# Attention 1: one 512-column value product per key block and head, collected into one burst per head pair

## The chip, the cores and the metric

The kernel runs on one core of one Trainium2 chip. The metric is device time in microseconds of one whole execution. Beside it stands one profiled execution, from which all durations below come.

## What is computed

The reference is one step of a two-layer transformer trunk. Layer 0 mixes tokens with multi-head latent attention, layer 1 with grouped-query attention; a mixture of experts follows each. The change touches layer 0's attention alone, cut here to its core:

```
def block_attention(q, k, v, scale):
    ...
    def one_block(qblk):
        s = jnp.einsum('bqhgd,bkhd->bhgqk', qblk, k).astype(jnp.float32) * scale
        p = jax.nn.softmax(s, axis=-1).astype(v.dtype)
        return jnp.einsum('bhgqk,bkhe->bqhge', p, v)
...
def mla_attend(q_nope, q_pe, keys, w_uk, w_uv, w_o):
    """Absorbed MLA: keys (B,Tk,KV_DIM) = [c_kv | k_pe] shared by all heads; values = c_kv."""
    ...
    k = keys[:, :, None, :]
    v = keys[:, :, None, :KV_LORA]
    o = block_attention(q, k, v, MLA_SCALE)[:, :, 0]
    o = jnp.einsum('bthc,chv->bthv', o, w_uv).reshape(B, T, MLA_HEADS * MLA_V)
    return o @ w_o
```

`qblk` holds 128 queries. The kernel first turns the latents into values per head (with `w_uv`), so the value product of a head has 64 numbers per key. There are 16 heads, 128 prompt tokens that see 128 keys, and 512 latent tokens that see 640 keys (five blocks of 128). Everything is float32.

## The kernel before

The queries come in five tiles of 128: tile 0 is the prompt, tiles 1 to 4 are the latents. Attention of layer 0 walks 80 steps. A head pair has ten of them, numbered here 0 to 9: two heads for each of the five tiles, so steps 0 and 1 are the prompt tile, 2 and 3 the first latent tile, and so on. There are eight pairs.

The softmax of a step is spread over three engines and two further steps. PE (TensorE) writes the scores (L1994); DVE takes the maximum (`peak`, L1139); ACT takes the exponential (`exp`, L721); DVE divides by the sum (`normalize`, L1146 and L1148). Two steps later PE transposes the result into one shared PSUM place (L1666), and ACT copies it to SBUF (L733). PE's program order is fixed: at step s it issues the scores of s, the transposes of s-2, a `hook`, and at even s a `pair`. The hook makes the next pair's keys and queries in PSUM bank 7 (`MAKE_AT`: keys, L1950, at steps 0 and 1; queries, L1957, at steps 3, 6, 7 and 8) and, at steps 2 and 9 (`ADA_AT`), one slice of layer 1's modulation (`ada`, L1686). `spare_free` waits until ACT and DVE have emptied bank 7 (ACT's part for keys is `key_out`, L771). ACT's part for a slice is `mod_out`: a copy (L693), then two DMA issues (L697).

`pair` is the value product (L1769). For one query tile and both heads of a pair it multiplies transposed probabilities, 128 columns at a time, by 64 columns of values, for every key block: 10 instructions for a latent tile, 2 for the prompt. The two heads of a pair write the lower and the upper 64 partitions of one PSUM bank, so each instruction uses one half of the array's columns. In the trace each float32 matmul appears as two passes, so 10 instructions are 20 rows. We call the ten instructions of one latent tile a group. Its results come from steps two earlier, so tile 1 is due at step 6, tile 2 at step 8, tile 3 at step 0 of the next pair and tile 4 at step 2 of the next pair. The prompt's two instructions are due at step 4.

After the last group DVE copies the result (`latent_out`, L1128), and PE starts the output projection (`mix`, L1741), which needs the weights `w_wo0` and `w_wo1`. At the same time ACT fetches two gate rows (L715) and layer 1's first modulation sums (`mod_fetch`, L709 and L712); DVE finishes these (L1058 to L1062), and PE transposes them (`turn_mods`) between the projections of tiles 0 and 1.

SP's queue issues weight loads in program order. The slices of layer 1's modulation alternate between two SBUF places, slots 0 and 1. `w_wo0` is loaded before attention, `w_wo1` in the second last pair, the first two experts' weights (L485) after the last slice is made.

Of the kernel before, what the change touches and what calls it, by code (L numbers as in the profile page):

```python
# [96 lines left out]


Q_TURN_AT = (0, NTILE + 1)

NQ, NK = HEADS * HD, KVH * HD
SCALE = (QD ** -0.5, HD ** -0.5)
# [77 lines left out]
def program(nc, ctx, A, O):  # L180
# [98 lines left out]
    xn = [lambda t, o=o: ar(o + (t % 2) * D, D) for o in (21120, 23040)]  # L279
    hT = [lambda t, o=o: ar(o + (2 + t % 2) * D, D) for o in (21120, 23040)]  # L280
    Pb = ar(17280, 2 * LKEYS)
    PT = ar(18560, 4 * LKEYS)

    W_PT = ((ar(18944, NB * QW), ar(18944 + NB * QW, NB * QW)), (ring(12288, NB * QW), ring(12288 + NB * QW, NB * QW)))
    W_PP = ring(12288 + 2 * NB * QW, 2 * P)
# [39 lines left out]
        keys = step(s)[3]  # L325
        return 4 * BANK if s % 2 == 0 else 6 * BANK if keys == P else 6 * BANK - P

    def ptbuf(s, n):
        return PT[:, (s % 4) * LKEYS:(s % 4) * LKEYS + n]

    def pt_out_g(s):

# [4 lines left out]
        return split(W_PT[half][h % 2], NB)[:, :, at * P:(at + 1) * P]  # L337


    PV0 = PAIR * NTILE  # L340
    CTX, HALF = 1, (2, 3)

    def wide_done(m, part):
        return PV0 + 3 * m + part
# [17 lines left out]
    def half_bank(half):  # L362
        return bank(7, QW, half * QW)

    def oT_out(it):

        return bank(7, P) if it == 0 else bank(6, P, (it - 1) * P)

    def oT_block(l, m, it, n=1):
        at = m * TOK + it * P  # L370
        return oT[l][:, at:at + n * P]
# [3 lines left out]
        return bank(6 + j % 2 if j < ADA_0 else 7, ADA_ITEMS[j][2])  # L375

    def ada_slot_of(j):
        return ADA_SLOT[j] if j < ADA_0 else (j - ADA_0) % 2

    def ada_at(j):  # L380

# [86 lines left out]
    def _(sp):  # L468
# [59 lines left out]

        def experts(l):

            load_gu(l, 0)
            if l:
                sp.wait_ge(S("qk_ready"), NTILE + 2)
                rows_e_in(1)
                sp.wait_ge(S("pv_done"), wide_done(PAIR - 1, HALF[1]))
            load_gu(l, 1)
            sp.wait_ge(S("mixed"), NTILE * (l + 1))
            load_dn(l, 0)
            load_gu(l, 2)
            load_dn(l, 1)  # L540
            load_dn(l, 2)
            if l == 0:
                mod_fetch(1, 1)
            sp.wait_ge(S("h_ready"), NTILE * (l + 1))
            for v in range(2):
                sp.dma_start(gate_m[:, v * D:(v + 1) * D], modrow[l][v, 5:6, :].broadcast_to([P, D])).then_inc(S("gates_m"), 16)
            sp.wait_ge(S("routed"), l + 1)
            for e in range(NE - RING_N):
                end = end_of(e)
                sp.wait_ge(S("gu_done", l), end)  # L550
                load_gu(l, e + RING_N)
# [27 lines left out]
            load_ada(j)  # L579
        sp.wait_ge(S("ada_made"), 1 + max(j for j in range(ADA_0) if ada_slot_of(j) in (3, 4)))  # L580
        load(S("uq_landed"), w_uq, A["mla_w_uq"], 3)
        sp.wait_ge(S("ada_made"), ADA_0 - 2)
        load(S("wo_landed", 0), w_wo0, A["mla_w_o"][0], KD)
        for j in range(ADA_0, ADA_ALL):
            load_ada(j)
            if j == ADA_0 + 1:
                mod_fetch(0, 1)
            if j == ADA_0 + 3:
                mod_store(0)
        sp.wait_ge(S("made"), len(MAKES) * PAIR)  # L590
        load(S("wo_landed", 0), w_wo1, A["mla_w_o"][1], KD)
        rows_e_in(0)
# [72 lines left out]
    def _(act):  # L665
# [58 lines left out]
        def heads(hook):  # L724

            for s in range(STEPS + 2):
                if s >= 2:
                    j = s - 2
                    keys = step(j)[3]
                    act.wait_ge(S("p_turned"), j + 1)  # L730
                    if j >= 4:
                        act.wait_ge(S("pv_done"), (j - 4) // 2 + 1)
                    act.activation(ptbuf(j, keys), ps[:, 4 * BANK:4 * BANK + keys], ACT.Copy).then_inc(S("pt_ready"), 1)  # L733
                if s < STEPS:
                    exp(0, s)
                    hook(0, *divmod(s, PER_PAIR))
# [304 lines left out]
    def _(dve):  # L1041
# [77 lines left out]

        def prompt_out(l, m):  # L1120

            dve.wait_ge(S("pv_done"), wide_done(m, CTX) if l else m * NTILE + 1)
            nc.vector.tensor_copy(oT_block(l, m, 0), bank(7, P)).then_inc(S("oT_prompt"), 1)

        def latent_out(m):

            dve.wait_ge(S("pv_done"), m * NTILE + NTILE)
# [534 lines left out]
    def _(pe):  # L1662
# [92 lines left out]

        def heads(score, v_of, hook):

            def pair(p):

                m, it = divmod(p, NTILE)  # L1760
                blocks, first = (1, 5) if it == 0 else (LKEYS // P, 0)
                pe.wait_ge(S("pt_ready"), 2 * p + 2)
                if it == 0:
                    spare_free(m, PROMPT_AT)
                if m and it == 1:
                    pe.wait_ge(S("oT_latent"), m)
                for j in range(blocks):
                    for odd in range(2):
                        last = mm(oT_out(it)[VD * odd:VD * (odd + 1)], v_of(2 * m + odd, first + j),  # L1769
                                  ptbuf(2 * p + odd, blocks * P)[:, j * P:(j + 1) * P], start=j == 0, stop=j == blocks - 1)  # L1770
                last.then_inc(S("pv_done"), 1)

            for s in range(STEPS + 4):
                if s < STEPS:
# [14 lines left out]
                if s >= 4 and s % 2 == 0:  # L1789
                    pair((s - 4) // 2)  # L1790

        def heads_g(score, v_of, last_turns):

# [531 lines left out]
```

## Time and profile before

| | |
|---|---|
| median of three runs | 1293.39 us (1291.4 to 1294.76) |
| profiled execution | 1292.7 us, of which span 1290.9 us |
| PE busy | 1231.8 us, 95% of the span |
| attention of layer 0 | from about 138 to 392 us |
| TensorE clock granted there | 1.00 of full speed |

The span runs from the first to the last instruction of the profiled execution; the execution's own time is 1.8 us more. A row of the timeline merges neighbouring instructions of one line on one engine; its second number is how long they are busy, and the start of the following row says when the engine went on.

### The profile page before, as it was taken

What the parts mean: (1) busy time and instruction counts of PE and PEld (TensorE: products, weight loads), DVE (VectorE), ACT (ScalarE), POOL (GpSimd) and SP (SyncE); (2) the same over time, 40 slices, a digit from 0 to 9 for tenths busy, and PEclk for the clock granted to TensorE, in tenths of its full rate; (3) what the DMA queues carried; (4) which work ended last, traced back from release to release, by engine and by line L of the source; (5) the groups of instructions that cost most, each with busy time, mean ns of one, the idle gap of its engine ahead of it and who ended that gap; (6) DMA issues with size and microseconds to landing.
All of it is one profiled execution on the core that took longest, in us unless ns stands there. A gap on an engine that the chain in (4) does not pass through costs nothing.

```text
span 1290.9 us, 17251 instructions
## 1 busy us (share of the span) xinstructions
PE 1231.8 (95%) x5561; PEld 681.9 (53%) x5562; DVE 589.3 (46%) x1338; ACT 409.8 (32%) x855; POOL 58.2 (5%) x63
## 2 busy tenths in 40 slices
PE   7999999999999999998978999799999999999997
PEld 4554566666664475443434444466654574444443
DVE  1322455555552574322228544888735663322216
ACT  2332344444451121111022325677732111111122
POOL 0103000000000020000002000000000110000002
PEclk9999999999999999999998999899999999999999
DMA  9979999622244057999987000600020279999947
GB/s 373 414 312 407 414 413 410 259 100 100 100 186 165 33 202 244 355 355 356 364 313 267 9 1 9 256 1 1 2 99 0 102 274 317 355 293 334 352 183 265
DMA packets 88357, 290.18 MB, mean 225 GB/s; under 512 B 9209, under 2 KB 27580, under 8 KB 86876
## 3 DMA queue, kind: packets, MB, share of 16 engines
q1 hardware_dynamic: 46032, 185.68, 39.4%
q0 software_dynamic: 16640, 64.59, 12.7%
q10 hardware_dynamic: 25612, 38.96, 8.9%
q8 instruction: 42, 0.69, 0.2%
q14 instruction: 31, 0.25, 0.1%
HBM read 214.48 MB, written 74.73 MB: 224 GB/s over the span
## 4 chain that ended last, share of the span: by engine, by line
PE 80%; DMA 6%; DVE 5%; ACT 3%; SPq 3%; issue 2%; ACTq 1%; DVEq 1%; POOL 0%; POOLq 0%
PE ps L2114 16%; PE ps L1724 11%; PE ps L1741 10%; PE ps L2143 7%; PE ps L1666 7%; PE ps L1994 6%; PE ps L1957 4%; PE ps L1769 3%; PE ps L2193 3%; PE ps L1818 3%; PE ps L1686 2%; DMA arena<-in_moe_gu 2%; PE ps L2056 2%; PE ps L1950 2%; PE ps L1967 2%
## 5 line engine op out<-in xcount | busy, mean ns | idle before, releaser
L2114 PE MATMUL ps<-arena 128*128 (+1 forms) x560 | 247.7, 595 | 0.0
L2114 PEld LDWEIGHTS ps<-arena 128*128 128x128 f32 x560 | 104.5, 191 | 118.1 <-issue 118.0
L1666 PE MATMUL ps<-const,arena 128*128 128x128 f32 (+2 forms) x1000 | 145.4, 279 | 18.0 <-DMA const<-in_const 8.2
L1724 PE MATMUL ps<-arena 128*128 128x512 f32 (+2 forms) x400 | 152.1, 535 | 4.6 <-DVE arena L1246 1.2
L1666 PEld LDWEIGHTS ps<-const,arena 128*128 128x128 f32 (+2 forms) x1000 | 115.8, 142 | 76.6 <-issue 39.8
L1139 DVE TENSOR_REDUCE hst<-ps 128x1 f32<-128x640 f32 (+1 forms) x160 | 110.9, 714 | 94.0 <-PE ps L1994 80.1
L1741 PE MATMUL ps<-arena 128*128 128x512 f32 x320 | 142.0, 597 | 1.4 <-issue 1.4
L2143 PE MATMUL ps<-arena 128*128 (+1 forms) x280 | 126.1, 593 | 2.2 <-ACT arena L844 2.2
L721 ACT ACTIVATE arena<-ps,hst 128x640 f32<-128x640 f32 (+1 forms) x160 | 112.4, 706 | 42.0 <-DVE hst L1139 42.0
L1724 PEld LDWEIGHTS ps<-arena 128*128 128x128 f32 x400 | 74.4, 190 | 74.1 <-issue 58.1
L1741 PEld LDWEIGHTS ps<-arena 128*128 128x128 f32 x320 | 59.1, 190 | 69.8 <-issue 69.7
L1994 PE MATMUL ps<-arena 128*128 128x320 f32 (+1 forms) x288 | 90.3, 432 | 1.4 <-issue 1.4
L2143 PEld LDWEIGHTS ps<-arena 128*128 128x128 f32 x280 | 53.0, 190 | 68.7 <-issue 68.7
L733 ACT ACTIVATE arena<-ps 128x640 f32<-128x640 f32 (+1 forms) x80 | 49.4, 618 | 120.6 <-PE ps L1666 112.8
L1148 DVE TENSOR_SCALAR arena<-arena,hinv 128x640 f32<-128x640 f32 (+1 forms) x160 | 80.0, 500 | 13.1 <-issue 0.9
L831 ACT ACTIVATE arena<-ps 128x256 f32<-128x256 f32 x35 | 13.4, 383 | 226.5 <-PE ps L2114 207.3
L1549 DVE STREAM_TRANSPOSE arena<-arena 128x1024 f32<-128x1024 f32 x31 | 62.9, 2028 | 35.9 <-DMA arena<-slot_rows 35.9
L1555 DVE TENSOR_TENSOR arena<-ps,arena 128x256 f32<-128x256 f32 x35 | 14.8, 422 | 132.9 <-ACT arena L831 132.9
L1994 PEld LDWEIGHTS ps<-arena 128*128 128x128 f32 x288 | 50.0, 189 | 28.5 <-issue 13.7
L844 ACT ACTIVATE arena<-ps 128x1024 f32<-128x1024 f32 x33 | 33.8, 1023 | 96.1 <-PE ps L2143 96.1
L2193 PE MATMUL ps<-arena 64*128 64x320 f32 (+1 forms) x288 | 54.2, 458 | 6.1 <-ACT arena L721 5.5
L1957 PE MATMUL ps<-arena 128*128 128x320 f32 x192 | 57.0, 433 | 0.0
(218 smaller groups left out, 1173.9 us busy)
## 6 DMA issues: line engine op xcount, KB each, us to landing
arena<-in_moe_gu SPq DMA_DIRECT2D x128, 512.0 KB, 13.1
arena<-in_ada_w SPq DMA_DIRECT2D x62, 768.0 KB, 11.9
slot_rows<-arena POOLq DMA_DIRECT2D x10, 4096.0 KB, 67.7
arena<-in_moe_w_down SPq DMA_DIRECT2D x64, 512.0 KB, 16.1
slot_rows<-arena ACTq DMA_DIRECT2D x33, 512.0 KB, 8.5
arena<-slot_rows ACTq DMA_DIRECT2D x124, 128.0 KB, 13.4
arena<-mod_rows SPq DMA_DIRECT2D x12, 512.0 KB, 12.3
arena<-in_gqa_w_qkv SPq DMA_DIRECT2D x12, 512.0 KB, 13.7
```

The costliest lines, as they stand in the source:

```text
L721: act.activation(split(pbuf(l, s, keys), 2 if keys > P else 1), scores(s, keys), ACT.Exp, bias=hst[:, b:b + 1], accum_out=hsum[:, b:b + 1] ...
L1139: nc.vector.tensor_reduce(hst[:, b:b + 1], scores(s, step(s)[3]), AX.XY, ALU.max, negate=True)\
L1148: nc.vector.tensor_scalar(pbuf(l, j, keys), pbuf(l, j, keys), hinv[:, b:b + 1], None, ALU.mult)\
L1549: nc.vector.transpose(e_xsT[:, c].rearrange("p (k r b) -> p k r b", k=KD, b=XB), e_xs[:, c].rearrange("p (r a k) -> p k r a", k=KD, a=XB)) ...
L1666: return nc.tensor.transpose(out, in_, ident[0:rows, 0:rows])
L1724: last = mm(bank(2 + b, cols), hT[l](t)[:, k * P:(k + 1) * P], w[:, k], start=k == 0, stop=k == KD - 1)
L1741: last = mm(bank(mix_bank(it) + half), oT_block(l, k, it), w[:, k], start=k == 0, stop=k == KD - 1)
L1957: last = mm(bank(7, QCH), w[:, k, h * P:(h + 1) * P], m_qlT[:, at:at + QCH], start=k == 0, stop=k == 2)
L1994: last = mm(scores(s, keys)[:, c], m_qT[:, at:at + P], m_kT[:, k:k + w], start=True, stop=True)
L2114: last = mm(bank(gu_bank(u)), e_xsT[:, nth(u, D)][:, k * P:(k + 1) * P], w(k * BANK, BANK), start=k == 0, stop=k == KD - 1)
L2143: last = mm(bank(6 + n), e_hidT[:, nth(u, FF)][:, k * P:(k + 1) * P], w(k * D + n * BANK, BANK), start=k == 0, stop=k == 1)
L2193: last = mm(scores(s, keys)[:, c], g_qT[half, q:q + P], g_kT[half, at:at + w], start=True, stop=True)
```

## The change

The four latent tiles of a pair share one product. ACT writes the transposed probabilities of the four tiles beside each other, so that a key block of one head is 512 columns (`pt_out_m`, buffers `M_PT` and `M_PP`). PE then issues ten instructions of 512 columns for the pair, all at step 2 of the next pair, in place of four groups of ten with 128 columns at steps 6, 8, 0 and 2. The prompt's two instructions stay at step 4. ACT's copies wait for the previous pair's product.

The second buffer takes SBUF that was slot 0. So the slices use slots 2 and 1, `w_wo0`, which lies on slot 2, is loaded after the last slice there, and the first experts' weights wait for the last value product.

```diff
+LATENTS_AT = ((2, 0, NB),)
...
-    PT = ar(18560, 4 * LKEYS)
+    M_PT, M_PP = (ar(18560, NB * BANK), ring(10240, NB * BANK)), ring(12800, 2 * P)
...
+    def pt_out_m(s):
+
+        m, it, h, keys = step(s)
+        if it == 0:
+            return M_PP[:, (h % 2) * P:(h % 2 + 1) * P]
+        return split(M_PT[h % 2], NB)[:, :, (it - 1) * P:it * P]
...
-        return ADA_SLOT[j] if j < ADA_0 else (j - ADA_0) % 2
+        return ADA_SLOT[j] if j < ADA_0 else 2 - (j - ADA_0) % 2
...
+            if l == 0:
+                sp.wait_ge(S("pv_done"), PV0)
             load_gu(l, 0)
...
-        sp.wait_ge(S("ada_made"), ADA_0 - 2)
-        load(S("wo_landed", 0), w_wo0, A["mla_w_o"][0], KD)
...
+        sp.wait_ge(S("ada_made"), 1 + max(j for j in range(ADA_ALL) if ada_slot_of(j) == 2))
+        load(S("wo_landed", 0), w_wo0, A["mla_w_o"][0], KD)
...
-                    if j >= 4:
-                        act.wait_ge(S("pv_done"), (j - 4) // 2 + 1)
-                    act.activation(ptbuf(j, keys), ps[:, 4 * BANK:4 * BANK + keys], ACT.Copy).then_inc(S("pt_ready"), 1)
+                    if m:
+                        act.wait_ge(S("pv_done"), latent_done(m - 1) if it else prompt_done(m - 1))
+                    turned = ps[:, 4 * BANK:4 * BANK + keys]
+                    act.activation(pt_out_m(j), split(turned, NB) if it else turned, ACT.Copy).then_inc(S("pt_ready"), 1)
...
-            def pair(p):
...
+            def latents(m, first, end):
+
+                if first == 0:
+                    pe.wait_ge(S("pt_ready"), (m + 1) * PER_PAIR)
+                    if m:
+                        pe.wait_ge(S("oT_latent"), m)
+                for j in range(first, end):
                     for odd in range(2):
-                        last = mm(oT_out(it)[VD * odd:VD * (odd + 1)], v_of(2 * m + odd, first + j),
-                                  ptbuf(2 * p + odd, blocks * P)[:, j * P:(j + 1) * P], start=j == 0, stop=j == blocks - 1)
-                last.then_inc(S("pv_done"), 1)
+                        last = mm(bank(6)[VD * odd:VD * (odd + 1)], v_of(2 * m + odd, j), M_PT[odd][:, j * BANK:(j + 1) * BANK],
+                                  start=j == 0, stop=j == NB - 1)
+                if end == NB:
+                    last.then_inc(S("pv_done"), 1)
```

PE's order changes at steps 6, 8, 0 and 2. Here are its instructions from the scores of step 8 to the group at step 0 of the next pair, before (64x128 is a group):

```order
L1994 MATMUL ps<-arena 128x320 x2
L1666 MATMUL ps<-const,arena 128x128 x5
L1957 MATMUL ps<-arena 128x320 x3
L1769 MATMUL ps<-arena 64x128 x10
L1994 MATMUL ps<-arena 128x320 x2
L1666 MATMUL ps<-const,arena 128x128 x5
L1686 MATMUL ps<-arena,cond 2x384 x8
L1994 MATMUL ps<-arena 128x128
L1666 MATMUL ps<-const,arena 128x128 x5
L1950 MATMUL ps<-arena 128x384 x2
L1769 MATMUL ps<-arena 64x128 x10
```

The same stretch in the changed kernel, with its own line numbers:

```order
L2015 MATMUL ps<-arena 128x320 x2
L1676 MATMUL ps<-const,arena 128x128 x5
L1978 MATMUL ps<-arena 128x320 x3
L2015 MATMUL ps<-arena 128x320 x2
L1676 MATMUL ps<-const,arena 128x128 x5
L1696 MATMUL ps<-arena,cond 2x384 x8
L2015 MATMUL ps<-arena 128x128
L1676 MATMUL ps<-const,arena 128x128 x5
L1971 MATMUL ps<-arena 128x384 x2
```

The groups behind the queries of step 8 and behind the keys of step 0 are gone, so the next scores follow the makes directly. At PE's step 2 the row of the last group was this, between the slice and the scores of step 3:

```order
L1994 MATMUL ps<-arena 128x320 x2
L1666 MATMUL ps<-const,arena 128x128
L1686 MATMUL ps<-arena,cond 2x384 x8
L1769 MATMUL ps<-arena 64x128 x10
L1994 MATMUL ps<-arena 128x320 x2
```

And in the changed kernel:

```order
L2015 MATMUL ps<-arena 128x320 x2
L1676 MATMUL ps<-const,arena 128x128
L1696 MATMUL ps<-arena,cond 2x384 x8
L1785 MATMUL ps<-arena 64x512 x10
L2015 MATMUL ps<-arena 128x320 x2
```

The ten instructions stay where they were and become four times as wide; they now hold all four latent tiles of the previous pair.

On SP's queue, the end of the attention part before is this (the last slice, the second half of the output weights, modulation rows, the router, the experts' weights):

```order
L473 DMA arena<-in_ada_w 128x1536
L474 DMA arena<-in_ada_w 128x1536
L473 DMA arena<-in_mla_w_o 128x2048
L474 DMA arena<-in_mla_w_o 128x2048
L526 DMA arena<-mod_rows 128x1024 x4
L527 DMA rw<-in_moe_router 128x256
L485 DMA arena<-in_moe_gu 128x1024 x8
```

And in the changed kernel:

```order
L480 DMA arena<-in_ada_w 128x1536
L481 DMA arena<-in_ada_w 128x1536
L480 DMA arena<-in_mla_w_o 128x2048
L481 DMA arena<-in_mla_w_o 128x2048
L480 DMA arena<-in_mla_w_o 128x2048
L481 DMA arena<-in_mla_w_o 128x2048
L533 DMA arena<-mod_rows 128x1024 x4
L534 DMA rw<-in_moe_router 128x256
L492 DMA arena<-in_moe_gu 128x1024 x8
```

Both halves of the output weights now stand behind the last slice, and the wait for the last value product stands ahead of the experts' weights.

## Rows read from the trace of the kernel before

**Rows 1.** The page: busy time, share of the span and instructions of PE.

```profile
PE 1231.8 (95%) x5561; PEld 681.9 (53%) x5562; DVE 589.3 (46%) x1338; ACT 409.8 (32%) x855; POOL 58.2 (5%) x63
```

**Rows 2.** Windows, middle and last pair; columns: length, PE, PEld, DVE, ACT, POOL, clock, DMA.

```profile
264.44:296.76 32.32, 32.32 (x230) 21.68 (x227) 16.68 (x38) 14.97 (x36) 0.00 (x0) 1.00 0.28 100
361.44:391.93 30.49, 27.82 (x249) 19.02 (x245) 14.90 (x35) 16.17 (x37) 0.00 (x0) 1.00 0.65 237
```

**Rows 3.** Waits in that middle pair: total us, times, longest.

```profile
ACT arena L733 <- PE ps L1666: 16.2, 10, 3.2
```

**Rows 4.** Timeline of PE, steps 7 and 8 of a pair.

```profile
255.02 1.78 PE L1957 MATMUL ps<-arena 128*128 128x320 f32 x6
256.64 1.24 PE L1994 MATMUL ps<-arena 128*128 128x320 f32 x4
...
258.26 1.78 PE L1957 MATMUL ps<-arena 128*128 128x320 f32 x6
259.97 1.31 PE L1769 MATMUL ps<-arena 128*64 128x128 f32 x20
261.21 1.34 PE L1994 MATMUL ps<-arena 128*128 128x320 f32 x4
```

**Rows 5.** Timeline of PE: 64-row products of 128 and 256 columns, full ones of 512.

```profile
246.40 0.44 PE L1769 MATMUL ps<-arena 128*64 128x128 f32 x4
...
406.52 14.00 PE L1741 MATMUL ps<-arena 128*128 128x512 f32 x32
...
421.23 3.60 PE L1741 MATMUL ps<-arena 128*128 128x512 f32 x8
...
826.08 1.52 PE L1818 MATMUL ps<-arena 128*64 128x256 f32 x12
...
830.05 1.08 PE L1818 MATMUL ps<-arena 128*64 128x256 f32 x8
```

**Rows 6.** Timeline of PE and ACT, steps 9, 0 and 1.

```profile
265.09 1.00 ACTq L697 DMA_DIRECT2D mod_raw<-arena  x2
266.20 0.70 ACT L733 ACTIVATE arena<-ps 128x640 f32<-128x640 f32 x1 [1.14 <-PE ps L1666]
266.78 1.31 PE L1769 MATMUL ps<-arena 128*64 128x128 f32 x20
267.14 0.47 ACT L771 ACTIVATE arena<-ps 64x384 f32<-64x384 f32 x1
268.89 1.46 PE L1950 MATMUL ps<-arena 128*128 128x384 f32 x4
```

**Rows 7.** Timeline of PE, last pair: slice of step 2, scores of steps 5 to 7.

```profile
365.93 1.47 PE L1686 MATMUL ps<-arena,cond 128*2 128x384 f32 x16
...
372.61 1.34 PE L1994 MATMUL ps<-arena 128*128 128x320 f32 x4
...
374.33 1.24 PE L1994 MATMUL ps<-arena 128*128 128x320 f32 x4
...
377.51 1.34 PE L1994 MATMUL ps<-arena 128*128 128x320 f32 x4
```

**Rows 8.** The chain that ended last, from 384 to 410 us: start, us, what.

```profile
387.39 0.71 ACT arena L733
...
388.24 0.76 PE ps L1666 x5
...
389.77 1.34 PE ps L1769 x20
...
394.05 10.23 DMA mod_vec<-in_vec_m
...
406.35 0.24 PE ps L1666
```

**Rows 9.** SP's timeline, and DMA issues from 361 to 405 us with landing times.

```profile
385.76 5.99 SPq L485 DMA_DIRECT2D arena<-in_moe_gu  x8
...
arena<-in_mla_w_o SPq DMA_DIRECT2D x2, 1024.0 KB, 9.3
```

More of the change, by code:

```diff
@@ L326, in turned_at @@
         return 4 * BANK if s % 2 == 0 else 6 * BANK if keys == P else 6 * BANK - P
-    def ptbuf(s, n):
-        return PT[:, (s % 4) * LKEYS:(s % 4) * LKEYS + n]
+    def pt_out_m(s):
[3 more added lines that the diff above has]
+        return split(M_PT[h % 2], NB)[:, :, (it - 1) * P:it * P]
     def pt_out_g(s):
@@ L337, in pt_out_g, with prompt_done, latent_done @@
         return split(W_PT[half][h % 2], NB)[:, :, at * P:(at + 1) * P]
-    PV0 = PAIR * NTILE
+    PV0 = 2 * PAIR
     CTX, HALF = 1, (2, 3)
+    def prompt_done(m):
+        return 2 * m + 1
+    def latent_done(m):
+        return 2 * m + 2
     def wide_done(m, part):
@@ L363, in half_bank @@
         return bank(7, QW, half * QW)
-    def oT_out(it):
-        return bank(7, P) if it == 0 else bank(6, P, (it - 1) * P)
     def oT_block(l, m, it, n=1):
@@ L728, in heads @@
                     j = s - 2
-                    keys = step(j)[3]
+                    m, it, _, keys = step(j)
                     act.wait_ge(S("p_turned"), j + 1)
-                    if j >= 4:
-                        act.wait_ge(S("pv_done"), (j - 4) // 2 + 1)
-                    act.activation(ptbuf(j, keys), ps[:, 4 * BANK:4 * BANK + keys], ACT.Copy).then_inc(S("pt_ready"), 1)
+                    if m:
+                        act.wait_ge(S("pv_done"), latent_done(m - 1) if it else prompt_done(m - 1))
+                    turned = ps[:, 4 * BANK:4 * BANK + keys]
+                    act.activation(pt_out_m(j), split(turned, NB) if it else turned, ACT.Copy).then_inc(S("pt_ready"), 1)
                 if s < STEPS:
@@ L1120, in prompt_out @@
         def prompt_out(l, m):
-            dve.wait_ge(S("pv_done"), wide_done(m, CTX) if l else m * NTILE + 1)
+            dve.wait_ge(S("pv_done"), wide_done(m, CTX) if l else prompt_done(m))
             nc.vector.tensor_copy(oT_block(l, m, 0), bank(7, P)).then_inc(S("oT_prompt"), 1)
         def latent_out(m):
-            dve.wait_ge(S("pv_done"), m * NTILE + NTILE)
+            dve.wait_ge(S("pv_done"), latent_done(m))
             nc.vector.tensor_copy(oT_block(0, m, 1, LAT), bank(6)).then_inc(S("oT_latent"), 1)
@@ L1756, in heads, with prompt @@
         def heads(score, v_of, hook):
-            def pair(p):
[L1760 to L1767, printed above, removed]
+            def prompt(m):
+                pe.wait_ge(S("pt_ready"), m * PER_PAIR + 2)
+                spare_free(m, PROMPT_AT)
+                for odd in range(2):
+                    last = mm(bank(7, P)[VD * odd:VD * (odd + 1)], v_of(2 * m + odd, NKEYT - 1), M_PP[:, odd * P:(odd + 1) * P],
+                              start=True, stop=True)
+                last.then_inc(S("pv_done"), 1)
[5 more added lines that the diff above has]
+                for j in range(first, end):
                     for odd in range(2):
-                        last = mm(oT_out(it)[VD * odd:VD * (odd + 1)], v_of(2 * m + odd, first + j),
-                                  ptbuf(2 * p + odd, blocks * P)[:, j * P:(j + 1) * P], start=j == 0, stop=j == blocks - 1)
-                last.then_inc(S("pv_done"), 1)
+                        last = mm(bank(6)[VD * odd:VD * (odd + 1)], v_of(2 * m + odd, j), M_PT[odd][:, j * BANK:(j + 1) * BANK],
+                                  start=j == 0, stop=j == NB - 1)
+                if end == NB:
+                    last.then_inc(S("pv_done"), 1)
             for s in range(STEPS + 4):
@@ L1788, in heads @@
                     hook(*divmod(s, PER_PAIR))
-                if s >= 4 and s % 2 == 0:
-                    pair((s - 4) // 2)
+                m, r = divmod(s, PER_PAIR)
+                if m < PAIR and r == PROMPT_AT:
+                    prompt(m)
+                for at, first, end in LATENTS_AT:
+                    if m and r == at:
+                        latents(m - 1, first, end)
         def heads_g(score, v_of, last_turns):
```

## The prediction

> **What bounds the kernel now.** I read the page first: PE is busy for 95% of the span [rows 1], so the question for attention 1 is whether PE's time there is work or waiting. The windows answer it. In a middle pair PE is busy for all of 32.32 us while DVE has 16.68 and ACT 14.97 [rows 2]. Pairs 1 to 6 read alike in the timeline, step by step. The waits say the same from the other side: in that pair ACT's copies alone waited 16.2 us for PE's transposes [rows 3]. So in pairs 0 to 6 a microsecond less of PE is a microsecond less of time, until one of the softmax steps behind it becomes late. The last pair is another matter: it makes no keys or queries for a successor, and PE is busy for 27.82 of the 30.49 us up to the projection [rows 2]. Its end is a chain of single steps, read below from the chain of waits.
>
> **What a group costs.** A group of 20 passes begins at 259.97, and the scores behind it begin at 261.21: 1.24 us. That is not all. The same six passes of a query make take 1.62 us until the next instruction starts when scores follow (255.02 to 256.64), and 1.71 us when a group follows (258.26 to 259.97). The scores take 1.34 us behind a group and 1.24 us behind a make [rows 4]. So 0.09 us ahead and 0.10 us behind also belong to the group; I take 1.43 us as what disappears with it.
>
> **What the burst costs.** The trace has no 64-row product of 512 columns, so I bound it from three widths. At 128 columns 20 passes are busy 1.31 us [rows 4] and 4 passes 0.44 us [rows 5]: 0.87 us for 16 more, or 0.109 us for two passes (one of each head, side by side in the two halves of the array). At 256 columns 12 passes take 1.52 and 8 take 1.08: 0.22 us for two. A full-width pass of 512 columns takes (14.00 - 3.60) / 24 = 0.433 us [rows 5]. The cost is proportional to columns, and two half-width passes cost one full one. So ten steps of two passes grow by 10 x (0.43 - 0.109) = 3.21 us, and the burst takes 1.24 + 3.21 = 4.45 us. From below, four times 0.109 would give 4.50; a price of 0.22 doubled gives 4.55, an excess of 3.31. I keep 3.21. The slice is ahead of it and the scores are behind it as before, so no edge is added.
>
> The columns therefore cost the same: four groups stream as much as one burst. What is gained is three sets of edges. Each group spends 1.24 - 10 x 0.109 = 0.15 us of its own on starting and ending, plus 0.19 on its neighbours, 0.34 together. The Trainium skill (TensorEngine Tiling, Tiling Modes, Key Properties) says that changing the tiling mode drains the engine; TensorE: Matmul & The Clock Gate (Part 2, step by step) puts a drain at some 128 cycles, as an estimate 0.05 us at 2.4 GHz, which for a change on either side would be 0.11 us a group in place of 0.34. The rows decide here.
>
> **Where the removed groups stood.**
> - Steps 6 and 8 of pairs 0 to 6: 14 groups, each behind a query make, with the next step's make behind them. That make needs bank 7 emptied by DVE, and the next scores (1.24) and transposes cover that copy (a like one of ACT takes 0.47 [rows 6]). 14 x 1.43 = 20.0 us.
> - Step 0 of pairs 1 to 6: 6 groups, behind the first key make. Here something waits. ACT issues two stores of the slice of step 9 until 266.09, so its copy of step 8 starts only at 266.20, and its `key_out` ends at 267.61. PE's second key make needs that, and starts at 268.89 now [rows 6]. Without the group it would be ready at 268.89 - 1.43 = 267.46; ACT and a hand-over of under 0.1 us allow it at about 267.7. So 1.2 us comes back, 0.2 turns into a wait: 6 x 1.2 = 7.2 us. Bounds: 1.43 each if ACT catches up, 0.9 if the transposes ahead wait as well.
> - Step 0 of pair 7: no keys are made, and the transposes of step 9 wait for the same late copy. Nothing.
> - Steps 6 and 8 of pair 7: step 5, without a group, takes 372.61 to 374.33 = 1.72 us, and step 6 with one 374.33 to 377.51 = 3.18 [rows 7]. If steps 6 to 9 run at 1.7 to 1.75, the two groups give 2.8 us; DVE with 14.90 us and ACT with 16.17 in this window of ten steps [rows 2] need 1.5 and 1.6 us a step, so they just keep up.
> - The groups at steps 0 and 2 behind the last pair. ACT's copy of step 78 starts at 387.39, held up by the stores of the last slice; the transposes of step 79 start at 388.24, and the last product at 389.77 [rows 8]. Tile 3's group lay inside that wait: removing it gives nothing. The last product becomes the burst.
>
> **The sum.** Gains: 20.0 + 7.2 + 2.8 = 30.0 us. Bursts: seven at step 2 of pairs 1 to 7 and one at the end, 8 x 3.21 = 25.7 us. Net -4.3 us.
>
> **What moves and costs nothing.** The burst holds PE for 4.45 us; behind it wait only scores of step 3 and transposes whose inputs are long ready, and DVE's `latent_out` stands at step 4. ACT's new wait (for the previous burst) is on copies of step 2, whose transposes PE issues at step 4, behind the burst. The wider stride of ACT's copy has its like in layer 1: same 128x640 elements there, no dearer. Both halves of the output weights now leave SP after the slice at step 2 of the last pair. That slice begins at 365.93 and takes 1.5 us [rows 7], the projection begins at 391.93 [rows 2]; with the burst in between and the last pair's gain off, some 25 us are left. One half took 9.3 us to land [rows 9]; two behind each other, under 20. The experts' weights (385.76 now) start 5.4 us later against the last product's end (389.77 + 1.34 [rows 8]); they are first multiplied behind all five projection tiles of 14.00 us [rows 5].
>
> What has least room is the fetch behind the last product: its last piece is issued at 394.05 and takes 10.23 us; the small transposes at 406.35 come behind it, 0.45 us after PE ran dry [rows 8]. In the changed kernel the eight loads of experts' weights, 5.99 us of issuing [rows 9], start together with it and no longer ahead of it. Either can win: from -0.45 (fetch sooner, no wait) to +5.4 us (fetch behind all of them). I take no change, since both queues share the engines now too.
>
> The profiled execution took 1292.7, so -4.3 gives 1288.4; the median of the runs shown is 0.7 above it, so **1289.1 us**.
>
> **Rivals.**
> - *The edges aren't saved.* If the 0.34 us belongs to the neighbours' own rhythm, a removed group gives 1.09: 14 x 1.09 + 6 x 0.9 + 2 x 1.05 = 22.8 against 25.7, time about 1296.3. Against: scores and makes without a group show no such edge [rows 4]. That is within 0.3% of before. Chance 0.12. With the Trainium skill's drains (the estimate above, 0.11 us for each of the 22) it would be about 1294.
> - *The fetch falls behind the experts' weights.* 5.4 us later than now would make it 1294.5; half of that 1291.8. Within 0.3%. Chance 0.10.
> - *Slower: the groups were cover for the softmax.* Removing them shortens steps 7, 9 and 1 against the chain maximum, exponential, scaling, transposes, copy. If that chain is late by w in each of the 22 places that count, the sum is -4.3 + 22 w; it is nil at w = 0.20 and slower by over 0.3% from w = 0.37, for instance w = 0.5 gives 1300. For: step 1 shows such a lateness. Against: at steps 7 and 9 a make or a slice of 1.4 to 1.6 us remains, and DVE and ACT are idle half the pair [rows 2]. Chance 0.04.
> - *Slower: the output weights land late*, which takes under 170 GB/s for 4.2 MB in 25 us; one half alone needed 9.3 us in company [rows 9]. At 120 GB/s PE waits 10 us: 1299. Chance 0.02.
>
> **How the numbers follow.** The forecast's mechanism has the remaining 0.72. Within it the bounds are: 1.43 at step 0 (-1.4) and no fetch wait (-0.45) below, 1285 to 1287; the dearer burst (+0.8) and 0.9 at step 0 (+1.8) above, 1291.7. The range, with the runs' own spread of some 1.5 us, is 1285.5 to 1292.5; it leaves out the first rival's upper part and the slower ones. 0.3% of 1293.4, about what a measurement of this kernel can tell from no change, is 3.9 us, so the line stands at 1289.5 and the forecast lies just past it. Of the 0.72 I give 0.56 to faster and 0.16 to the same; with the rivals: faster 0.56, same 0.39, slower 0.05.
>
> **What would show it.** Right: pair length 32.3 falls to about 31.5; the 20 passes of 512 columns take 4.4 to 4.5 us; scores of steps 7 and 9 take 1.24 us; a wait of 0.1 to 0.3 us for ACT ahead of the second key make; PE idle for most of the 1.3 us that tile 3's last group filled. Wrong: new waits at steps 7 to 9, a pass pair far from 0.43, or a wait over 1 us at the small transposes between the first two projection tiles.

## The result, and the profile after

The changed kernel is slightly slower. Its median is 1295.2 us (1293.5 to 1298.1, 8 runs) beside 1292.1 us for the kernel before (8 runs): ratio 1.0026, 95% interval 1.0016 to 1.0036. Run again later it gave 1296.1 against 1291.8: 1.0031 (1.0022 to 1.0040). The forecast was 1289.1, its range 1285.5 to 1292.5: wrong. The profiled execution took 1293.8 us, span 1292.0.

PE's line of the page beside [rows 1]: 480 matmuls and 480 weight loads less, 6.0 us less busy, and a span 1.1 us longer.

```profile
PE 1225.8 (95%) x5081; PEld 660.6 (51%) x5082; DVE 589.7 (46%) x1338; ACT 410.3 (32%) x855; POOL 58.3 (5%) x63
```

The windows answer to [rows 2]: from step 2 to step 2 of the next pair, first an early pair, then the one that now holds [rows 2]'s stretch, then the last pair up to the projection (length, PE, PEld, DVE, ACT, POOL, clock, DMA share, GB/s):

```profile
167.96:200.28 32.32, 31.57 (x167) 19.06 (x166) 16.76 (x38) 14.99 (x34) 0.00 (x0) 1.00 1.02 413
264.17:295.72 31.55, 31.55 (x168) 19.06 (x167) 16.67 (x38) 14.99 (x34) 0.00 (x0) 1.00 0.29 100
...
359.55:390.06 30.51, 26.60 (x137) 12.73 (x130) 12.46 (x27) 13.12 (x27) 0.00 (x0) 0.94 0.56 216
```

The later pair fell from 32.32 to 31.55 us, as forecast. The early one did not fall at all: PE is busy for 31.57 us and waits for 0.75. And the last one ran at a mean granted clock of 0.94.

PE's timeline in the later pair shows the burst, and at its end two query makes with scores directly behind them:

```profile
265.45 1.48 PE L1696 MATMUL ps<-arena,cond 128*2 128x384 f32 x16
266.85 4.51 PE L1785 MATMUL ps<-arena 128*64 128x512 f32 x20
271.30 1.34 PE L2015 MATMUL ps<-arena 128*128 128x320 f32 x4
...
284.71 1.24 PE L2015 MATMUL ps<-arena 128*128 128x320 f32 x4
...
286.33 1.78 PE L1978 MATMUL ps<-arena 128*128 128x320 f32 x6
287.95 1.24 PE L2015 MATMUL ps<-arena 128*128 128x320 f32 x4
```

The burst holds PE for 271.30 - 266.85 = 4.45 us, the forecast's number. A make takes 287.95 - 286.33 = 1.62 us and the scores 1.24, without the 0.09 and 0.10 that a group cost its neighbours [rows 4].

The early pair, ACT and PE from step 9 to step 1 (compare [rows 6]):

```profile
163.22 1.81 ACTq L706 DMA_DIRECT2D mod_raw<-arena  x2
...
165.08 0.70 ACT L743 ACTIVATE arena<-ps 128x640 f32<-128x640 f32 x1 [1.89 <-issue]
...
165.93 0.74 PE L1676 MATMUL ps<-const,arena 128*128 128x128 f32 x5 [0.71 <-ACT arena L743]
...
166.03 0.47 ACT L781 ACTIVATE arena<-ps 64x384 f32<-64x384 f32 x1
...
166.60 1.53 PE L1971 MATMUL ps<-arena 128*128 128x384 f32 x4
```

ACT spends 1.81 us on issuing the slice's two stores, so its copy starts late and PE's transposes wait 0.71 us. The kernel before has this row too, in the early pair that [rows 6] does not show:

```profile
168.11 1.84 ACTq L697 DMA_DIRECT2D mod_raw<-arena  x2
```

In the later pair of the changed kernel the same two stores take 1.03 us:

```profile
260.16 1.03 ACTq L706 DMA_DIRECT2D mod_raw<-arena  x2
261.29 0.70 ACT L743 ACTIVATE arena<-ps 128x640 f32<-128x640 f32 x1 [1.16 <-PE ps L1676]
```

The windows suggest what differs: the DMA engines are full in the early pair (share 1.02, 413 GB/s) and at 0.29 in the later one. Around the stores themselves (160 to 166 and 258 to 264 us) the share is 1.03 and 0.57. Pairs 1 to 3 are all like the early one and pairs 4 to 6 all like the later one, in both kernels; no run changed the DMA load alone, so that it is the cause is not shown.

The end of attention, in the chain that ended last (start, us, what), answers to [rows 8]; behind it PE's timeline with its two waits, and the clock of the last burst's stretch (columns as in the windows above):

```profile
380.65 0.71 ACT arena L743
...
381.50 0.75 PE ps L1676 x5
...
382.27 0.71 ACT arena L743
...
383.03 6.19 PE ps L1785 x20
389.22 0.84 issue
390.06 13.97 PE ps L1751 x32
404.03 0.17 PE ps L1676
```

```profile
381.50 0.74 PE L1676 MATMUL ps<-const,arena 128*128 128x128 f32 x5 [1.84 <-ACT arena L743]
383.03 1.98 PE L1785 MATMUL ps<-arena 128*64 128x512 f32 x4 [0.79 <-ACT arena L743]
```

```profile
383.03:389.31 6.28, 6.19 (x20) 1.71 (x20) 0.04 (x1) 0.00 (x0) 0.00 (x0) 0.73 0.00 0
```

The last burst took 6.19 us where its like takes 4.51. The granted clock fell to the lower of its two levels (1.2 GHz) at 383.03, for part of the burst (0.73 over the stretch). What went ahead of it on PE is a wait of 1.84 us, 0.74 us of transposes and a wait of 0.79 us. The small transposes at 404.03 follow the projection at once: the fetch that was to have least room was in time.

From the first score to the projection, attention took 253.75 us, against 253.61 before. So the result is not made in attention alone: three microseconds stand at the end of the program. There POOL gathers the experts' rows while the last are still being stored, DVE scales what was gathered by its weight, and PE sums it. From PE's first sum to its last this took 31.75 us, where it had been 28.71. PE's first and last rows of it, before and after:

```profile
1256.01 7.28 PE L2201 MATMUL ps<-X,const 128*128 128x512 f32 x16
1279.40 5.31 PE L2201 MATMUL ps<-arena,const 128*128 128x512 f32 x12
...
1254.13 7.03 PE L2222 MATMUL ps<-X,const 128*128 128x512 f32 x16
1280.56 5.31 PE L2222 MATMUL ps<-arena,const 128*128 128x512 f32 x12
```

The first gather already lands late. From POOL's issue of it to DVE's first scaling 4.89 us passed before, and 8.00 now:

```profile
1255.82 0.97 POOL L660 DMA_INDIRECT arena<-slot_rows,slot_i  x1 [205.91 <-DMA slot_rows<-arena]
1260.71 1.28 DVE L1593 SCALAR_TENSOR_TENSOR arena<-arena 128x1024 f32<-128x1024 f32 x1 [8.86 <-DMA arena<-slot_rows,slot_i]
...
1254.64 0.97 POOL L669 DMA_INDIRECT arena<-slot_rows,slot_i  x1 [206.58 <-DMA slot_rows<-arena]
1262.64 1.28 DVE L1603 SCALAR_TENSOR_TENSOR arena<-arena 128x1024 f32<-128x1024 f32 x1 [12.67 <-DMA arena<-slot_rows,slot_i]
```

POOL's fourth gather waited 2.54 us for the last stores before. Now it waits 5.45, and the view names nothing that it waits for:

```profile
1261.84 0.97 POOL L660 DMA_INDIRECT arena<-slot_rows,slot_i  x1 [2.54 <-DMA slot_rows<-arena]
...
1263.58 1.17 POOL L669 DMA_INDIRECT arena<-slot_rows,slot_i  x1 [5.45 <-issue]
```

A smaller excess stands between the two layers, where the last expert of layer 0 is gathered: PE's gap there is 10.93 us in place of 9.97.

These excesses add up to 4.1 us, and the span grew by 1.1 only. Of the difference 2.0 us lie ahead of attention, where it was the kernel before that lost its clock for a while, at 105.8, behind two waits of PE (0.80 and 1.19 us) that the changed kernel has as well (0.81 and 1.20): its first score came at 138.32 us, the changed kernel's at 136.31. The stretch from 106 to 140 us, before and after (the granted clock is the third number from the end):

```profile
106.00:140.00 34.00, 32.64 (x86) 16.52 (x86) 7.05 (x10) 8.10 (x14) 10.16 (x12) 0.95 1.02 410
106.00:140.00 34.00, 32.21 (x90) 16.59 (x89) 8.26 (x14) 9.05 (x17) 10.18 (x12) 1.00 0.97 382
```

This fall comes in 4 of the 14 traces below, of either kind of kernel. Another 0.9 us lie between the projection and layer 0's last expert; what made them was not followed up.

### The profile page after: what moved, and what is told of

It is laid out like the page before. It is cut to its first block, busy times and chain, and to the rows that moved or that the text cites. A ratio compares the mean times of both kernels' runs of the same rounds, so it can differ in the third digit from the quotient of the medians.

```text
span 1292.0 us, 16286 instructions
## 1 busy us (share of the span) xinstructions
PE 1225.8 (95%) x5081; PEld 660.6 (51%) x5082; DVE 589.7 (46%) x1338; ACT 410.3 (32%) x855; POOL 58.3 (5%) x63
## 4 chain that ended last, share of the span: by engine, by line
PE 78%; DMA 7%; DVE 4%; ACT 4%; SPq 3%; issue 2%; ACTq 1%; DVEq 1%; POOLq 0%
PE ps L2135 15%; PE ps L1734 11%; PE ps L1751 11%; PE ps L1676 7%; PE ps L2164 6%; PE ps L2015 6%; PE ps L1978 4%; DMA arena<-in_moe_gu 4%; PE ps L1839 3%; PE ps L1785 3%; PE ps L2214 3%; PE ps L2077 2%; PE ps L1696 2%; PE ps L1988 2%; PE ps L1971 1%
## 6 DMA issues: line engine op xcount, KB each, us to landing
arena<-in_moe_gu SPq DMA_DIRECT2D x128, 512.0 KB, 12.8
```

## Experiments

The ratio is to the kernel before, timed beside each; its median there was 1292.1, 1291.8 or 1291.7 us. Attention is counted from the first score to the projection, the gap from the last product of layer 0's experts to PE's next instruction, the sums as above, all in the one profiled execution.

| kernel | median us (n) | ratio, 95% interval | attention | gap | sums |
|---|---|---|---|---|---|
| before | 1292.1 (33) | | 253.6 | 10.0 | 28.7 |
| changed | 1295.2 (8) | 1.0026, 1.0016 to 1.0036 | 253.75 | 10.9 | 31.75 |
| changed, again | 1296.1 (12) | 1.0031, 1.0022 to 1.0040 | 252.1 | 11.1 | 30.9 |
| loads alone | 1291.8 (11) | 0.9998, 0.9989 to 1.0007 | 253.6 | 10.1 | 28.8 |
| deferred stores, pairs | 1291.6 (11) | 0.9996, 0.9987 to 1.0005 | 247.9 | 11.7 | 32.3 |
| deferred stores, all | 1289.8 (11) | 0.9982, 0.9973 to 0.9991 | 246.9 | 11.1 | 31.1 |
| products in the tail | 1291.4 (11) | 0.9991, 0.9982 to 1.0000 | 252.1 | 12.3 | 28.4 |
| before, 64 instructions | 1295.6 (6) | 1.0031, 1.0019 to 1.0043 | 253.6 | 11.1 | 31.2 |
| changed, 112 instructions | 1297.6 (5) | 1.0044, 1.0031 to 1.0057 | 253.9 | 10.9 | 28.85 |
| changed, 64 instructions | 1290.4 (11) | 0.9990, 0.9981 to 0.9999 | 252.1 | 10.5 | 28.2 |
| before, deferred stores | 1291.6 (11) | 0.9995, 0.9986 to 1.0004 | 252.8 | 10.1 | 28.4 |
| three repairs | 1286.7 (5) | 0.9957, 0.9944 to 0.9970 | 247.7 | 10.5 | 28.4 |
| two repairs | 1286.7 (5) | 0.9958, 0.9945 to 0.9972 | 247.6 | 11.4 | 28.1 |
| two repairs, burst in two | 1287.65 (5) | 0.9964, 0.9950 to 0.9978 | 249.4 | 12.8 | 28.4 |

**The loads alone.** The kernel before with the changed places and times of the slices, the output weights and the experts' weights, and its value products as they were.

```diff
-        return ADA_SLOT[j] if j < ADA_0 else (j - ADA_0) % 2
+        return ADA_SLOT[j] if j < ADA_0 else 2 - (j - ADA_0) % 2
...
+            if l == 0:
+                sp.wait_ge(S("pv_done"), PV0)
...
-        sp.wait_ge(S("ada_made"), ADA_0 - 2)
-        load(S("wo_landed", 0), w_wo0, A["mla_w_o"][0], KD)
...
+        sp.wait_ge(S("ada_made"), 1 + max(j for j in range(ADA_ALL) if ada_slot_of(j) == 2))
+        load(S("wo_landed", 0), w_wo0, A["mla_w_o"][0], KD)
```

> The kernel before, with the change's loads only: modulation slices on slots 2 and 1, both halves of the output weights behind the slice at step 2 of the last pair, the first experts' weights behind the last value product; the value products stay four groups. If only PE's stalls in attention 1 explain the result, this runs as before (within 1 us), with attention 1 as long as before. If the moved loads hold the missing part of the 3 us, this is 2 to 3 us slower than before, and the trace shows a later landing behind the last value product.

1291.8 us and 253.6 us of attention: the moved loads cost nothing by themselves, and the rivals built on them fall.

**Deferred stores.** The changed kernel, with the stores of the slice of step 9 issued behind the key copy of the next step 1, so that ACT copies for PE first.

```diff
-                    mod_out(j)
+                    mod_out(j, r == ADA_AT[1] and m + 1 < PAIR)
...
+            if l == 0 and m and r == 1:
+                raw_store(ada_in(0, m - 1)[1])
```

> The changed kernel, with ACT's two stores of the step 9 slice issued behind the key copy of the next pair's step 1, in pairs 0 to 6; the last pair is untouched. If those stores make the second key make late, steps 0 and 1 together fall to 4.3 us in pairs 1 to 6 (from 5.4 in pairs 1 to 3 and 4.7 after), and the time falls by 1.1 x 3 + 0.4 x 3 = 4.5 us against the changed kernel. If the lateness comes from the softmax chain itself (maximum, exponential, scaling), the two steps keep at least 4.7 us and the time falls by under 2 us.

Attention fell to 247.9 us, 4.2 less than in the second trace of the changed kernel, where the clock held as it did here. From step 2 to step 2 every pair takes 31.35 us, early ones too; the windows of the kernel with two repairs, which has the same pairs, show it:

```profile
170.00:201.35 31.35, 31.35 (x168) 19.03 (x166) 16.67 (x38) 14.95 (x35) 0.00 (x0) 1.00 1.02 413
263.77:295.13 31.36, 31.36 (x171) 19.03 (x167) 16.66 (x38) 15.11 (x35) 0.00 (x0) 1.00 0.29 102
```

Steps 0 and 1 take 4.46 us in each. So the wait there was the stores, not the softmax chain. But the median was only 0.5 us below before, where attention was 5.7 shorter: sums of 32.3 us and a gap of 11.7 took most of it back.

**All stores deferred**, the last pair's behind the last copies too (without the condition on `m`, and one more line behind the walk: `raw_store(ADA_ALL - 1)`).

> As the kernel with deferred stores, and the last pair's two stores too are issued behind the last copies. If ACT's stores are what holds the end up, copy 78 starts 1.0 us sooner, PE's idle stretch ahead of the last burst falls from 1.84 to about 0.8 us, the clock holds, and the time falls by a further 1.0 us, or 2.7 with the clock: 5.5 to 7 us below the changed kernel, 2.5 to 4 below before. If the stores merely move, and delay the fetch of modulation sums behind the last product, the gain at the end is given back as a wait at the small transposes.

1289.8 us: 5.4 below the changed kernel and 2.3 below before, just short of what was expected. Attention is another 1.0 us shorter, PE's wait ahead of the last burst's transposes fell from 1.84 to 0.89 us, and the clock held; but it held with the longer wait as well, in the kernel with the last pair untouched. The sums stand at 31.1.

**Products in the tail.** The changed kernel with 8 and 3 products of the identity in PE's two waits ahead of the last burst. They compute nothing that is used.

```diff
+                if s in (STEPS, STEPS + 1):
+                    keep_busy((8, 3)[s - STEPS], 0)
```

> The changed kernel, with 8 and 3 products of the identity with itself on PE while it waits in the last two softmax steps, into a PSUM bank that nothing reads: extra work. If the last burst's 6.19 us (against 4.45 in the other pairs) is the clock, which fell to half as PE had idled ahead of it, the burst takes 4.45 us at clock 1.00 and the time falls by 1.7 us against the changed kernel, or by less where that drop doesn't come in each execution. If it is the burst's place (its reads against other traffic), it stays near 6.2 us and nothing is gained.

The last burst took 4.51 us, and the median fell by 3.8 us. That is more than the 1.7 of the clock can be, and the table says where the rest is: the sums took 28.4 us, 3.4 less, while the gap grew by 1.4. The edit did two things, then, and the second was not meant: it added 44 instructions to PE's program.

**PE's code.** The trace lists DMA packets by queue, and one kind is instructions. The page of the changed kernel:

```profile
q8 instruction: 38, 0.62, 0.2%
```

There were 42 of these before. 960 instructions less on PE (480 matmuls, 480 weight loads) go with four pieces less, so this is PE's program, arriving in pieces of 0.62 MB / 38 = 16 KB while it runs. The Trainium skill (Runtime: NRT & Kernel Launch, Instruction fetch mechanics) says the same of an engine's code: blocks of 16 KiB, 256 instructions, on a queue of its own, and the cost of a boundary "mostly hidden". By that, 960 is 64 short of four blocks, and every later piece arrives at another place in the program. It does: the last one came at 1265.0 us before, 9 us behind the first sum, and at 1253.3 in the changed kernel, 0.8 us ahead of it. This is the DMA of the changed kernel in the ten microseconds around that point, 1251.1 to 1261.1 (the queue's packets, MB and share; then issues with KB each and median us to landing):

```profile
q8 instruction: 1, 0.02, 0.6%
...
arena<-in_final_norm ACTq DMA_DIRECT2D x1, 512.0 KB, 7.4
arena<-slot_rows,slot_i POOLq DMA_INDIRECT x3, 8.3
```

Four runs asked whether the piece makes the difference.

```diff
+        for _ in range(64):
+            pe.nop().then_inc(S("pad"), 1)
         pe.wait_ge(S("first_inputs"), 16 * len(first_inputs))
```

The kernel before with these 64 instructions, which only count up a semaphore:

> The kernel before with 64 such instructions at its start: 64 is what its code lacks to stand against the pieces as the changed kernel's does (960 + 64 = 4 x 256). Nothing else is changed. Theory (code pieces): the last piece arrives 10 to 12 us earlier than 1265.0, among the last expert's stores, the last sums take 31 to 32 us instead of 28.7 and the wait at layer 0's gathers 10.9 or more instead of 10.0; time 1292.1 + 3.2 + 0.9 = 1296. Rival (chance, or something of attention): 1292 as before.

1295.6 us, ratio 1.0031: a loss as large as the change's, on the unchanged value products. The last piece came at 1255.2, 0.8 us ahead of the first sum. The sums took 31.2 us, the gap 11.1. The same stretch of this kernel, 1253.0 to 1263.0, and POOL's wait:

```profile
q8 instruction: 1, 0.02, 0.6%
...
arena<-in_final_norm ACTq DMA_DIRECT2D x1, 512.0 KB, 7.6
arena<-slot_rows,slot_i POOLq DMA_INDIRECT x3, 8.5
```

```profile
1265.76 1.17 POOL L660 DMA_INDIRECT arena<-slot_rows,slot_i  x1 [5.77 <-issue]
```

The changed kernel with 112 of them:

> The changed kernel with 112 extra instructions on PE, which only count up a semaphore that nobody reads, while PE waits for its first inputs. The trace shows PE's code arriving in pieces of 16 KB (256 instructions of 64 bytes). In the three kernels whose last piece arrives while the last expert's rows are being stored and gathered (1253.3 in the changed kernel) the last sums take 31.1 to 32.3 us; where it arrives elsewhere (1265.0 before, 1242.4 with the products in the tail) 28.4 to 28.8. The change issues 960 instructions less, which is 64 short of four pieces, so all later pieces move. Theory (code pieces): 112 more instructions move the pieces out of both gather stretches; last sums back to about 28.5 us (-3.2), the wait at layer 0's gathers from 10.9 to about 10.0 us (-0.9), time about 1291.1. Rival (chance landing of stores and gathers, no relation to the code): both stay as they are, about 1295. A cost of the extra instructions at the start would show in the start of attention's first scores.

The sums went to 28.85 us as expected, but the time rose: the 112 instructions are not free. PE's first instruction behind them starts at 17.91 us, where it is 8.01 without any and 10.57 with 64. PE's first key makes started 7.5 us later than in the changed kernel (112.55 against 105.06), so this run speaks through its sums alone. The gap stayed at 10.9, where 10.0 was expected. Its last burst took 6.21 us at a lower clock, as in the changed kernel's first trace. With 64 in place of 112:

> The changed kernel with 64 counting instructions at the start in place of 112: in the kernel before 64 moved the first key makes by 0.5 us only, where 112 cost the changed kernel 7.5 us. Theory (code pieces): last piece about 1245, last sums 28.5 us; time 1295.7 - 2.9 + 0.5 = 1293.3. Rival (the pieces have no part in it): 1296.

1290.4 us, 4.8 and 5.8 below the changed kernel's two medians, and 3 below the forecast. Against the changed kernel's first trace 3.6 of it are in the sums, 0.4 in the gap and 1.6 in the last burst, less 0.8 for the start (105.87): 4.8. Against its second, whose burst kept its clock, the sums, the gap and the start give 2.8 only; that trace is of an execution 2 us below its kernel's median. The last piece came at 1238.6, 14 us ahead of the sums, and the stretch from 1250.0 to 1260.0 has no packet of instructions:

```profile
q10 hardware_dynamic: 576, 1.57, 40.8%
q0 software_dynamic: 246, 0.94, 33.0%
...
arena<-in_final_norm ACTq DMA_DIRECT2D x1, 512.0 KB, 5.4
arena<-slot_rows,slot_i POOLq DMA_INDIRECT x4, 6.0
```

```profile
1258.87 0.95 POOL L669 DMA_INDIRECT arena<-slot_rows,slot_i  x1 [2.54 <-DMA slot_rows<-arena]
```

Gathers land in 6.0 us where they took 8.3, the row of `in_final_norm` in 5.4 where it took 7.4, and POOL's wait is the 2.54 of the kernel before. And the changed kernel itself, once more:

> The changed kernel once more, unchanged, on the same chip as the padded one. If the excess behind attention is systematic: about 1295, last sums 31 to 32 us, last piece of code near 1253. If it was chance: last sums 28.5 us in this trace and a median nearer 1292. The granted clock in the last burst says whether the fall at the end of attention is the rule: 6.2 us again, or 4.5.

1296.1 us, last piece 0.8 us ahead of the sums, sums 30.9. The last burst took 4.51 us this time (window with columns as above), so the fall of the clock there comes in some executions and not in others, behind the same two waits; so far as the profiled ones go, in 2 of the 6 whose tail has no extra products, and in none of the 4 with them. That is too few to tell. But the mean granted clock is on record for every execution: it is below 0.990 in 12 of the changed kernel's 20 and in 1 of 11 with the products in the tail (before: in 12 of 72). Those 12 of the changed kernel average 1296.5 us, the other 8 1294.1. So its medians hold some 2 us that go along with the clock.

```profile
384.90:391.30 6.40, 5.45 (x23) 1.83 (x24) 0.69 (x1) 0.06 (x1) 0.00 (x0) 1.00 0.11 20
```

Over all fourteen traces: where the last piece arrives 0.8 us ahead of the first sum (five traces of four kernels), the sums take 30.9 to 32.3 us; where it arrives 8 to 9 us behind it or 12 to 19 ahead (nine), 28.1 to 28.9. In the two longest, 31.75 and 32.3, the granted clock also fell within the sums, behind PE's wait for the gathered rows (2.82 us in the changed kernel's first trace); without that the five stand at 30.9 to 31.2. The first gather parts them more sharply: 8.0 to 8.4 us from its issue to DVE's first scaling in the five, 4.8 to 5.0 in the nine. A mere shift in time does not do it: with deferred stores all this came 3 to 6 us earlier than in the changed kernel, and the piece, which moves along with the program, stood 0.8 us ahead again.

**The stores in the kernel before**, the same edit as in the changed one:

> The kernel before with the step 9 slices' stores issued behind the key copy of the next step 1 (the last one behind the last copies), PE's code unchanged. It asks how much of the repaired kernels' gain belongs to the stores alone. My theory: in the kernel before the group at step 0 covers the late copy, so in pairs 0 to 6 nothing or at most the 0.2 us a pair comes back; in the tail the copy of step 78 starts some 0.7 to 1.0 us earlier. Time 1290.5 to 1291.5, last sums 28.7 as before. Rival (the deferred stores are worth the same 5 us to either kernel, and value products have no part in it): about 1287.

1291.6 us, a shade above what was expected, its pairs still 32.33 us long. The group at step 0 had hidden the late copy; the change uncovered it.

**Repairs together.** Deferred stores, products in the tail and 72 counting instructions; then the same without the counting ones.

> The changed kernel with all three repairs: the stores of each step 9 slice issued behind the copies that PE waits for, 8 and 3 filler products in the two waits of the tail, and 72 counting instructions at the start. From the kernel with deferred stores alone (1289.8, last sums 31.1, wait at layer 0's gathers 11.1): code theory -2.6 and -1.1, about 1286.1; the filler products give 0 to -1.7 more, where the clock would have fallen. Rival (code has nothing to do with it): 1288 to 1290.

> The changed kernel with deferred stores and the 8 and 3 filler products in the tail, without counting instructions. The 11 fillers are 44 instructions of PE, which by the theory of the code pieces already move the last piece out of the last gather: last sums 28.4 us, wait at layer 0's gathers 10.5 to 12.3. Against the same with 72 counting instructions (1286.7, first key makes 1.1 us later) 0 to -1.1 from the start and 0 to +1.8 at layer 0's gathers: 1285.6 to 1287.4. Rival (the counting instructions were what helped): 1289.

1286.7 us both: 0.4% below the kernel before, and the fastest of all. The 44 instructions of the tail's products had already moved the last piece (13 us ahead of the sums).

**The burst in two parts**, same instructions, one more edge a pair:

```diff
-LATENTS_AT = ((2, 0, NB),)
+LATENTS_AT = ((2, 0, 3), (3, 3, NB))
```

> The repaired kernel with the burst in two parts: three key blocks at step 2 as now, two at step 3 behind the query make. Same passes, same columns, same number of instructions, so PE's code stands as in the repaired kernel; one more edge in each of seven pairs. If an edge costs the 0.34 us of the prediction: 7 x 0.34 = 2.4 us more than the repaired kernel, some 1289. Rival (edges cost nothing, what the groups cost was their columns): the same time as the repaired kernel.

PE's timeline of the split kernel, its second part at step 3 of a pair, and the window of the whole pair:

```profile
270.76 1.78 PE L1988 MATMUL ps<-arena 128*128 128x320 f32 x6
272.47 1.94 PE L1793 MATMUL ps<-arena 128*64 128x512 f32 x8
274.33 1.34 PE L2025 MATMUL ps<-arena 128*128 128x320 f32 x4
```

```profile
266.74:298.45 31.71, 31.71 (x171) 18.86 (x167) 16.66 (x38) 15.11 (x35) 0.00 (x0) 1.00 0.28 101
```

31.71 - 31.36 = 0.35 us for one edge, and the make ahead and the scores behind carry their 0.09 and 0.10 again (1.71 and 1.34 us). Six pairs lose that, 2.1 us. The last one, which has no query make at step 3, gains 0.3, and the trace's attention is 1.8 us longer. The medians differ by 1.0, less than five runs of each can tell apart, where 2.4 was expected. The price of an edge rests on the trace.

## Why the prediction was wrong

- **What the burst costs, and what a group costs: right.** 4.45 us, as forecast. From the scores of step 6 to the next pair's a pair saves 2.87 us (15.93 to 13.06), forecast 2.86. The split burst measures an edge at 0.35, forecast 0.34. The Trainium skill's drains, weighed in the prediction at 0.11 a group, are a third of that.
- **Last pair: right.** Its two groups gave the 2.8 us (8.07 to 5.30 over steps 6 to 8), and at step 0 nothing, as said.
- **"Step 0 of pairs 1 to 6: 6 x 1.2 = 7.2 us": the mechanism right, the size wrong.** The three later pairs give 1.08 each (5.74 to 4.66 over steps 0 and 1), the three early ones 0.32: together 4.2. I read the hold-up from one pair at 265 us, where the two stores take 1.00 us [rows 6], and held pairs 1 to 6 to be alike. On PE they are; on ACT the trace of the kernel before had 1.84, 1.80 and 1.78 us for the three early pairs. There PE's transposes wait too, and the bound of 0.9 was no bound. This is 3.0 us of the 4.3.
- **"The last product becomes the burst", 3.21 us: right at full clock**, 1.7 us more where the clock falls. That comes in some executions and not in others, and is not in the forecast at all.
- **What moves and costs nothing: right** (the loads alone, and the small transposes that wait for nothing).
- **The step that failed is the sum itself**: it ends at attention's end, as if what follows did not depend on the number of instructions ahead of it. With the numbers above attention gains 1.5 us at full clock (253.6 to 252.1), not 4.3. Then 960 instructions less on PE move its code's pieces, one into the stores and gathers of layer 0's last expert (+1.0, though here the piece's part is less sure) and one into those of layer 1's (+2.2 at full clock, +3.0 with the clock's fall in the sums). -1.5 + 1.0 + 2.2 gives +1.7 at full clock, and +4.2 where it falls in the last burst and in the sums; the medians say +3.1 and +4.3, and the 8 executions with a clock of 0.990 or more +2.0. The kernel before, given only the shift, loses 3.8 us; the changed kernel, given another, stands at 1290.4, inside the forecast's range.

None of the rivals was this. Two came near the time, and both are refuted by what they spoke of: the edges were saved (steps 6 to 9), so 1296.3 for edges not saved was not it, and the small transposes wait for no fetch, so neither was 1294.5. The lateness at step 1 that the cover rival named did come, behind the stores; at steps 7 and 9 there is none.

Left open: how one piece, 0.95 us on its queue, holds up gathers and loads for two to three. The runs show that moving it does this, and where, not by what: in the changed kernel it has arrived by 1254.3, ahead of the first gather's issue at 1254.64, which lands 3.1 us late all the same. The gap at layer 0 is less clean: 10.0 to 10.9 us with the piece 8 us or more ahead of it, 10.9 to 12.8 with it 1 to 3 us ahead.

## What to carry to other kernels

Price a wait that is about to be uncovered at its worst place, not at the one you happened to read: the same store issue took 1.0 us in one pair and 1.8 in another. When a change adds or drops instructions by the hundred, look at where the engine's own code arrives afterwards, above all at stretches that wait for DMA; 64 counting instructions during a start-up wait are a cheap test, and here went with 5 us. And an experiment that adds instructions tests their number too: the products in the tail looked like a proof of the clock, and half of what they gave came with the shift of code.

## What the runs showed of the hardware

- PE's program arrives in pieces of 16 KB during execution, 42 before and 38 after. Where a piece came 1.3 us ahead of the first of the last gathers, that gather took 8.0 to 8.4 us until its rows were used in place of 4.8 to 5.0, and the sums behind it 30.9 to 32.3 in place of 28.1 to 28.9. The Trainium skill's page quoted above (Runtime: NRT & Kernel Launch, Instruction fetch mechanics) has such a boundary mostly hidden; where PE is busy across the pieces the traces agree: in the changed kernel for 79.6 of the 80 us from 960 to 1040, with two pieces in them.
- A counting instruction on PE is not free: PE's first instruction behind them starts at 10.57 us with 64 and at 17.91 with 112, so one takes (17.91 - 10.57) / 48 = 0.15 us. Without any PE waits until 8.0 to 8.7 us for its inputs; so 64 moved the first key makes by 0.5 and 0.8 us only, 112 by 7.5.
- ACT is held for 1.81 us by issuing two stores in the pairs where the DMA engines' share is 1.02, for 1.03 us where it is 0.29 (1.03 and 0.57 around the stores themselves).
- Two half-width passes of 512 columns in two halves of the array take (4.45 - 0.15) / 10 = 0.43 us together, as one full-width pass does [rows 5].
